# Norm statistics of a two-block fp32 kernel: squares summed in four column groups instead of by full-width products or by VectorE adds

## The reference

```python
def layer_norm(x, g, b):
    xf = x.astype(jnp.float32)
    mu = jnp.mean(xf, axis=-1, keepdims=True)
    var = jnp.mean(jnp.square(xf - mu), axis=-1, keepdims=True)
    y = (xf - mu) * lax.rsqrt(var + LN_EPS)
    return (y * g.astype(jnp.float32) + b.astype(jnp.float32)).astype(x.dtype)
...
        x = layer_norm(ALPHA * x + 0.5 * swiglu(x, ffn1_w1[i], ffn1_w3[i], ffn1_w2[i]), ln1_g[i], ln1_b[i])
        proj = x @ w_in[i]
...
        x = layer_norm(ALPHA * x + merged @ w_out[i], ln2_g[i], ln2_b[i])
        x = layer_norm(ALPHA * x + 0.5 * swiglu(x, ffn2_w1[i], ffn2_w3[i], ffn2_w2[i]), ln3_g[i], ln3_b[i])
        ple = jax.nn.sigmoid(x @ ple_w_gate[i]) * (p[i] @ ple_w_proj[i])
        x = layer_norm(ALPHA * x + ple, ln4_g[i], ln4_b[i])
...
        h = rms_norm_2(x, norm_g[l]) * (1.0 + scale) + shift
```

## Time and profile before

| | us |
|---|---|
| median of 3 runs | 3131.28 (3130.58 to 3132.92) |
| profiled execution, its time | 3131.53 |
| profiled execution, its span | 3129.7 |
| mean granted clock of PE, share of full | 0.998 |
| busy: PE, DVE, ACT | 3082.8, 2368.0, 1222.6 |

### The profile page before, as it was taken

One profiled execution on the slowest core, in us unless ns is written; L12 is line 12 of the kernel. 1 busy time (PEld: TensorE's weight loads), 2 busy tenths in 40 slices (PEclk: granted clock), 3 DMA queues, 4 the chain that ended last, 5 costly groups with the idle time before them and its releaser, 6 DMA issues.

```text
span 3129.7 us, 37552 instructions
## 1 busy us (share of the span) xinstructions
PE 3082.8 (98%) x14712; PEld 2490.4 (80%) x14712; DVE 2368.0 (76%) x4017; ACT 1222.6 (39%) x1884; POOL 56.2 (2%) x49
## 2 busy tenths in 40 slices
PE   8999999999999999999999999999999999999998
PEld 6887888877988887777878888888777788788887
DVE  6777767778869678888598776767797789789736
ACT  4233323335342455554243233222366534534414
POOL 0000000000000001130000000000000000000000
PEclk9999999999999999999999999999999999999999
DMA  3222212223343351012212111111211221122242
GB/s 131 74 73 75 81 61 68 68 68 109 119 101 135 115 197 56 8 48 114 95 54 68 41 54 61 48 54 48 68 54 63 104 77 64 48 70 101 81 168 74
DMA packets 89247, 250.13 MB, mean 80 GB/s; under 512 B 8560, under 2 KB 24816, under 8 KB 87536
## 3 DMA queue, kind: packets, MB, share of 16 engines
q1 hardware_dynamic: 89072, 247.73, 23.5%
HBM read 203.65 MB, written 44.04 MB: 79 GB/s over the span
## 4 chain that ended last, share of the span: by engine, by line
PE 90%; DVE 7%; ACT 2%; issue 1%; DMA 0%; DVEq 0%; SPq 0%; ACTq 0%
PE PS L577 88%; PE PS L582 2%; DVE WS L2228 1%; DVE X L2236 1%; DVE XS L2236 1%; DVE HELD L2290 1%; DVE X L2228 1%; ACT XS L1345 0%; DVE COLB L3038 0%; DVE XSf L2228 0%; ACT XSf L1345 0%; DVE TMP L2228 0%; DMA RAW<-in_W 0%; DVE TMP L2232 0%; ACT WS L1345 0%
## 5 line engine op out<-in xcount | busy, mean ns | idle before, releaser
L577 PE MATMUL PS<-XS,WS 128*128 128x512 f32 (+1 forms) x6480 | 1513.8, 391 | 20.4 <-DVE XS L2228 9.5
L577 PEld LDWEIGHTS PS<-XS,WS 128*128 128x128 f32 x6480 | 1208.9, 188 | 297.8 <-issue 27.1
L577 PE MATMUL PS<-HS,WS 128*128 128x512 f32 x2208 | 511.0, 390 | 3.1 <-DVE TMP L2228 2.7
L577 PEld LDWEIGHTS PS<-HS,WS 128*128 128x128 f32 x2208 | 414.1, 188 | 93.1 <-DVE TMP L2228 3.5
L2228 DVE TENSOR_TENSOR WS<-RAW,WS 128x512 fp32r<-128x512 f32 (+1 forms) x398 | 346.9, 880 | 173.8 <-ACT WS L1345 173.2
L1345 ACT ACTIVATE WS<-RAW 128x512 fp32r<-128x512 f32 (+1 forms) x398 | 307.6, 779 | 398.7 <-PE PS L577 344.0
L2228 DVE TENSOR_TENSOR X<-PS,X 128x512 f32<-128x512 f32 x272 | 184.2, 688 | 101.8 <-PE PS L577 101.7
L2228 DVE TENSOR_TENSOR TMP<-TMP,PS 128x512 f32<-128x512 f32 x304 | 203.6, 682 | 61.5 <-PE PS L577 58.7
L577 PE MATMUL PS<-T,WS 128*128 128x512 f32 x960 | 230.6, 389 | 0.0
L577 PEld LDWEIGHTS PS<-T,WS 128*128 128x128 f32 x960 | 180.2, 188 | 37.4
L1345 ACT ACTIVATE TMP<-PS 128x512 f32<-128x512 f32 x144 | 85.0, 596 | 291.0 <-PE PS L577 274.4
(11 more groups left out here) (338 smaller groups left out, 3580.6 us busy)
## 6 DMA issues: line engine op xcount, KB each, us to landing
RAW<-in_W SPq DMA_DIRECT2D x263, 512.0 KB, 3.3
RAWX<-in_W SPq DMA_DIRECT2D x30, 512.0 KB, 3.3
DC<-TMP SPq DMA_DIRECT2D x32, 256.0 KB, 2.1
X<-in_xT SPq DMA_DIRECT2D x8, 512.0 KB, 8.9
DX<-X SPq DMA_DIRECT2D x2, 2048.0 KB, 8.4
DCZ<-CA SPq DMA_DIRECT2D x8, 512.0 KB, 4.1
DGA<-TMP SPq DMA_DIRECT2D x16, 256.0 KB, 2.3
DGB<-TMP SPq DMA_DIRECT2D x16, 256.0 KB, 3.1
```

What stands on the lines that cost most here:

```text
L577: done = d.matmul(out, l, r, start=first, stop=last)
```

## The change

All ten half-norms now sum their squares in the same way, with no adds on DVE. For each k-tile, four products (`quarter_sums`) each take a quarter of the tokens (128 columns) with 32 columns of `ones` and write rows 32g to 32g+31 and columns 0 to 127 of the bank. After eight k-tiles, row group g holds the sums of quarter g. The root and the reciprocal (`rstd_rows`) then work on 128 columns instead of 512, in a TMP tile. Four further f32 products (`spread`) bring them back: column 32g of the identity, repeated 128 times, picks the row of quarter g and writes it to all rows, columns 128g on, of the same bank. DVE's scalings read that bank instead of HELD or HX, so the bank is free only at the last scaling (y7). The steps of `side` are one more, so the hooks are moved, and HX is gone.

```diff
-SUMMED = ("ln1", 1), ("ln2", 0), ("ln2", 1), ("ln3", 1), ("ln4", 0)
...
     SQ = [at(f"SQ{k}", 154 + 4 * k, [128, 512], F32) for k in range(8)]
     GW = at("GW", 188.0625, [128, 3, 128], F32)
-    HX = at("HX", 184, [128, 2, 512], F32)
...
             for k in range(8):
-                if within and k == 4:
+                if within and k in within:
                     hook()
...
+        def quarter_sums(out, src, first, last):
+
+            return mms([(out[32 * g:32 * g + 32, 0:128], ones[:, 0:32], src[:, 128 * g:128 * g + 128], first, last)
+                        for g in range(4)])
+
+        def spread(name, h):
+
+            r = tmp("rs", name, h)
+            e.wait_ge(ve("rs", name, h), dma("const")("cols"))
+            mms([(var_bank(name, h)[:, 128 * g:128 * g + 128], ident[:, 32 * g:32 * g + 1].to_broadcast([128, 128]), r[:, 0:128], True, True)
+                 for g in range(4)]).then_inc(*mm.inc("rb", name, h))
+
         def norm(name, h):
             mean, var = (name, "mean", h), (name, "var", h)
...
-            banks.take(var, (ac, "rs", name, h))
-            yield
-            if (name, h) in SUMMED:
-                yield
-                e.wait_ge(ve(name, "sqs", 7, h), *banks.free(var))
-                mms([(bank(*var), ones[:], squares(name, 0, h), True, True)]).then_inc(*mm.inc(name, "var", 7, h))
-            else:
-                e.wait_ge(*banks.free(var))
-                for k in range(8):
-                    if k == 4:
-                        yield
-                    e.wait_ge(ac(name, "sq", k, h))
-                    mms([(bank(*var), ones[:], squares(name, k, h), k == 0, k == 7)]).then_inc(*mm.inc(name, "var", k, h))
-            yield
-            yield
+            banks.take(var, (ve, name, last_scaled(name), 7, h))
+            yield
+            e.wait_ge(*banks.free(var))
+            for k in range(8):
+                if k == 4:
+                    yield
+                e.wait_ge(ac(name, "sq", k, h))
+                quarter_sums(bank(*var), squares(name, k, h), k == 0, k == 7).then_inc(*mm.inc(name, "var", k, h))
+            yield
+            spread(name, h)
             yield
...
-                product8(us[m], h, use, "ln3", beside=True, within=n in (1, 2, 3, 8, 9, 10, 12) or None)
+                product8(us[m], h, use, "ln3", beside=True,
+                         within={1: (4,), 2: (4,), 3: (4, 7), 8: (4,), 9: (4,), 10: (4, 7), 12: (4, 7)}.get(n))
...
-                        if k == 4 and h == 0 and i < 2:
+                        if k == 4 and h == 0 and i in (0, 1, 2, 4):
                             next(steps)
...
-            tmps.take(use, (ve, *(end or use)))
+            tmps.take(use, (mm, "rb", name, h) if width == 128 else (ve, *(end or use)))
...
-            root(name, h, 1024, LN_EPS, mm(name, "var", 7, h))
+            root(name, h, 1024, LN_EPS, mm(name, "var", 7, h), width=128)
...
+        def rstd_rows(name, h):
+
+            r = tmp("rs", name, h)[:, 0:128]
+            e.wait_ge(ac("rs", name, h))
+            d.reciprocal(r, r).then_inc(*ve.inc("rs", name, h))
+
...
-            if (name, h) in SUMMED:
-                total = squares(name, 0, h)
-                for k in range(1, 8):
-                    e.wait_ge(ac(name, "sq", 0, h), ac(name, "sq", k, h), *([ve(name, "sqs", k - 1, h)] if k > 1 else ()))
-                    tt(total, total, squares(name, k, h), ALU.add).then_inc(*ve.inc(name, "sqs", k, h))
-            yield
-            e.wait_ge(ve(name, "c", 7, h))
-            rstd(name, h, s)
+            yield
+            rstd_rows(name, h)
             yield
...
-                e.wait_ge(ve("rs", name, h), ac(name, "sq", 7, h))
-                scaled = stt(x, x, col(name + "_g", k), s, ALU.mult, ALU.mult)
+                e.wait_ge(mm("rb", name, h), ac(name, "sq", 7, h), ve(name, "c", 7, h))
+                scaled = stt(x, x, col(name + "_g", k), var_bank(name, h), ALU.mult, ALU.mult)
```

More of the change, by code:

```diff
@@ L481, in var_bank, with last_scaled @@
         return bank(name, "var", h) if name in LNS else bank("sq", name, h)
+    def last_scaled(name):
+        return "y0" if name == "ln4" else "y"
     def out_part(p):
@@ L643, in merge_norm @@
             yield
-            banks.take(var, (ac, "rs", "ln2", h))
-            e.wait_ge(ve("ln2", "sqs", 7, h), *banks.free(var))
-            mms([(bank(*var), ones[:], squares("ln2", 0, h), True, True)]).then_inc(*mm.inc("ln2", "var", 7, h))
+            banks.take(var, (ve, "ln2", "y", 7, h))
+            e.wait_ge(*banks.free(var))
+            for k in range(8):
+                e.wait_ge(ac("ln2", "sq", k, h))
+                quarter_sums(bank(*var), squares("ln2", k, h), k == 0, k == 7).then_inc(*mm.inc("ln2", "var", k, h))
+            yield
+            spread("ln2", h)
             yield
@@ L680, in up @@
                         banks.take(use3, (ve, name, "mul", fi, h))
-                        product8(us[fi][0], h, use1, tag, within=h == 0)
+                        product8(us[fi][0], h, use1, tag, within=None if h else (4, 7) if fi else (4,))
                         product8(us[fi][1], h, use3, tag, within=None if h == 0 else False)
@@ L777, in latents @@
                 for k in range(8):
-                    if k == 4 and n in (1, 2, 3):
+                    if k == 4 and n in (1, 2, 3) or k == 7 and n == 3:
                         hook()
@@ L1104, in out_product @@
                 banks.take(use, (ve, *use))
-                product8(u, h, use, "mh", pair=mh_pair, beside=h == 1, within=m in (3, 6) and h == 1 or None)
+                product8(u, h, use, "mh", pair=mh_pair, beside=h == 1, within={3: (4,), 6: (4, 7)}.get(m) if h else None)
             us = [w.take() for _ in range(8)]
@@ L1119, in norm_h @@
             steps = norm("ln4", h)
-            for _ in range(3):
+            for _ in range(4):
                 next(steps)
                 yield
-            square_sum("h", h, 8, lambda k: SQ[k][:])
+            use = ("sq", "h", h)
+            banks.take(use, (ve, "hy", 7, h))
+            e.wait_ge(*banks.free(use))
+            for k in range(8):
+                e.wait_ge(ac("sq", "h", h, k))
+                quarter_sums(bank(*use), SQ[k], k == 0, k == 7).then_inc(*mm.inc("sq", "h", h, k))
+            yield
+            spread("h", h)
             yield
@@ L1966, in embed @@
             biased(0)
-            root("h", 0, 1024, RMS_EPS, mm("sq", "h", 0, 7))
+            root("h", 0, 1024, RMS_EPS, mm("sq", "h", 0, 7), width=128)
             gate(12)
@@ L2064, in mixer @@
                     biased(1)
-                    root("h", 1, 1024, RMS_EPS, mm("sq", "h", 1, 7))
+                    root("h", 1, 1024, RMS_EPS, mm("sq", "h", 1, 7), width=128)
                     for k in range(8):
@@ L3149, in part @@
                     ALU.add, ALU.subtract).then_inc(*ve.inc("xs", "h", k, h))
-            rstd("h", h, HX[:, h, :])
+            rstd_rows("h", h)
             for k in range(8):
-                e.wait_ge(ve("gc", 1), ve("rs", "h", h), ac("ln4", "y", k, h), *tmps.free(("hp", h, k)))
-                stt(tmp("hp", h, k), X[:, k, half(h)], GC[:, 0, k:k + 1], HX[:, h, :], ALU.mult, ALU.mult).then_inc(
+                e.wait_ge(ve("gc", 1), mm("rb", "h", h), ac("ln4", "y", k, h), *tmps.free(("hp", h, k)))
+                stt(tmp("hp", h, k), X[:, k, half(h)], GC[:, 0, k:k + 1], var_bank("h", h), ALU.mult, ALU.mult).then_inc(
                     *ve.inc("hy", k, h))
```

## The result

The kernel after takes 3144.84 us (median of 5 runs, 3144.33 to 3145.67) against 3131.7 us of the kernel before in the same session (5 runs). The ratio is 1.0042, with a 95% interval of 1.0027 to 1.0056: slower by 13.1 us. Its profiled execution took 3144.84 us (span 3142.9), so it stands for the median, and its span is 13.2 us over that of before.

A forecast was written before the change was run, and what follows sets the result against it. TensorE (PE), busy 98% of the span, was taken to bound the kernel. Terms 0 + 0.7 + 2.5 + 0.2 - 0.1 + 15.6 + 2.5 - 8.0 = +13.4 us on 3131.53 gave about 3145 us, range 3136 to 3158.

The forecast's parts named there:

- places 1: ln1 half 0, first ffn: last down group stands 4.9 us for y7, waits that go offset it; sum 0.
- place 5: ln3 half 0, second ffn: first gate product waits for y7, but waits for XS parts go; -0.1 us.
- place 6: ln3 half 1, gate stage: 11.5 us stop at n = 5 for y7, plus 2.7 for the clock; +15.6 us in all.
- place 7: ln4 and h half 0: dearer ln4 sums, cheaper h sums, PE standing about 3.1 us at the spread; +2.5 us.
- variant (E): Rival: the clock also falls at ln1 half 0 and ln3 half 0, +2.5 to +5 us; inside the main case's 0.62.
- place 2: ln1 half 1, latents: +2.9 us of PE work minus four waits of 2.6 in all, perhaps a spread wait; +0.7 us.
- Quarter sums and spread: Unit costs on PE: 1.4 us for 4 k-tiles, 2.4 for 8 in a row, 1.03 for a spread.
- place 3: ln2 half 0, merge: sums and spread dearer for PE, no wait before to give back; +2.5 us.
- places 2 and 4: 4 is ln2 half 1: +2.5 us minus about 2.3 of waits, +0.2; place 2 was +0.7.
- Place 8: ln4 and h half 1, last norm: shorter reciprocals and sums on the chain over DVE; -8.0 us.
- Rival (C): Quarter sums: only two column groups at once, +1.4 us at some six places, +8, 3153 us; chance 0.13.
- Rival (B): Quarter sums: column groups run one after another, each sum 4.3 us more, +35, 3180 us; chance 0.05.

The follow-up runs named there:

- skip5: Kernel after with one bank of the ring left out ahead of the gate product of n = 5: 3130.11 us, ratio to before 0.9996.
- warm: Kernel after with 48 useless products right ahead of the 11.1 us stop at n = 5: 3142.66 us, ratio to before 1.0034.
- recip3: Kernel before with the change at ln4 and h half 1 alone, their 128-column reciprocals made three times in a row: 3125.28 us, ratio to before 0.9979.
- gouter: Kernel after with quarter products of ln1, ln3 and ln4 issued one column group after the other: 3162.1 us (a single run).
- h0_late3: Kernel after, banks left out at n = 0 and n = 5, spread of h half 0 moved 18 products later: 3123.94 us, ratio to before 0.9975.
- last_only: Kernel before with the change made for ln4 half 1 and h half 1 alone: 3122.81 us, ratio to before 0.9972.
- skip3: Kernel after with banks left out at n = 0 and n = 5 (the one meant at ln1 was not): 3129.27 us, ratio to before 0.9992.

## Why the prediction was right, and where its steps were off

The time was 3144.84 where 3145 was said, and the sign and the chain were right, but that it came within 0.2 us is luck: the slow clock was 5.5 us more than its term, place by place the other terms were too dear by some 4 us, and 1.7 us came from stretches that the change doesn't touch.

**The wait for the bank (places 1, 5, 6).** Right. The stops at places 1 and 6 were predicted at 4.9 and 11.5 us and were 4.65 and 11.14; the one at place 5, for which no length was given, was 2.14, and the 1.99 us for the spread there were not in the prediction at all. Without the slow clock the two cost nothing, as its -0.1 has it. skip5 shows that place 6 is the bank. The working of y7 there, held by a weight part that waits for PE, holds too: in after VectorE stands 5.00 us idle between the reciprocal and this weight part, which ACT delivers late, having itself waited 4.89 us for PE:

```profile
2301.49 0.95 DVE L2316 RECIPROCAL TMP<-TMP 128x128 f32<-128x128 f32 x1 [1.65 <-ACT TMP L1365]
2307.44 1.23 DVE L2248 TENSOR_TENSOR WS<-RAW,WS 128x1024 fp32r<-128x1024 f32 x1 [5.00 <-ACT WS L1365]
2308.58 1.40 DVE L2256 SCALAR_TENSOR_TENSOR X<-X,COL,PS 128x512 f32<-128x512 f32 x2
...
2323.39 0.74 DVE L2256 SCALAR_TENSOR_TENSOR X<-X,COL,PS 128x512 f32<-128x512 f32 x1
```

**The clock (places 1, 5, 7).** This is the term that was too small. I counted it once, 2.7 us at place 6; it was 2.3 there (warm shows it apart), but also 2.5, 1.7 and 1.7 us behind the stops of 4.65, 2.14 and 3.81 us: 8.2 in all. I had the case for places 1 and 5 as variant (E) and left place 7 out. I also didn't see that the trace of before has such a piece itself, at 752 us in place 2.

**Quarter sums and spread.** Too dear. What a block costs has to be counted as the 6.9 us of the full sum were, with the tenths that its neighbours lose to it: from one block's start to the next with 12 products between them it is 3.95 us (2423.41 to 2427.36), so 1.23 us a block, of which 1.01 is its own. Eight k-tiles cost 1.88 and the same 0.22, so 2.1, and a spread 0.9. My sum for four groups at once gave 1.25 and 2.1, and the rows bear it out: 32 more instructions cost 0.87 us (1.01 to 1.88), so 0.027 each, a quarter of 0.104, and 0.36 is left for both switches where I had 0.4. The step that failed is the one behind it, where I took 1.4 and 2.4 to be nearer to the rate of two groups; the spread was 0.13 too dear too. That is 0.4 us at place 3, and as much or more at 2, 4 and 8. Rival (C), two groups at a time, is excluded by the 1.01 us.

**The waits that were to go (place 2).** Of four waits, 2.6 us in all, I expected none. In after three are left, 1.06, 0.39 and 0.39 us, for parts of XS. That place 2 came out at 0.2 us all the same, against a kernel before with full clock there, is, as far as the rows can be added up, owed to the cheaper sums and to the tenths that each stop costs beside its idle time, which I had left out (recip3).

**Rival (B) and the overlap rule.** The Trainium skill, "TensorE: Matmul & The Clock Gate", Part 3 (What overlaps and what doesn't), has weight loads overlap running products only where the row group differs. The 1.01 us a block, with one row group throughout, disagrees with a serial reading of it, and the measurement decides. gouter lies nearer to the rule, with 0.074 us an instruction where neighbours share the column group as well. The same part has 2.38x for three column tiles. Here a full sum of 6.9 us became 2.1, 3.3x for four. By tile that is 0.82 beside 0.79, so the trace agrees, with 128 moved columns where the page's row has 512.

**Place 7.** The stop ahead of the spread was 3.81 us where I said 3.1: since the sums and the earlier spread were cheaper than I had them, PE came to it sooner, while ACT's root (at 2387.78) stood behind the eight biased rows and a table load. Moving the spread behind 18 more products gave back what the place had cost: 63.12 us from mean to mean in h0_late3, 63.09 in before.

**VectorE's work.** It fell by 45 us where I said some 60: by the records 35 adds of 0.69 us and ten reciprocals 2.4 us shorter are 48. Outside the last norm it shows only in the waits that went at places 2 and 4.

**Place 8.** -8.8 where I said -8.0, alone -8.9 in last_only. The chain from the mean to y(h) became 29.3 us (2446.23 - 2416.97), where I had 30.05; the terms given for that number, taken whole, make about 27, and how much of the sums lies on the chain was left to judgement. PE's own work had the larger say: in after it waits only 0.36 us at the first part of XS.

**A stretch that nothing touches** gave 1.5 us between 763 and 1550. Two stops that both kernels have (1.94 us at 1095 in after, 1.33 us at 1450 in before) were each followed by a lower clock in one trace and not in the other, so they cancel. What is left is a wait at 1132, put down to instruction issue, which was 0.92 us instead of 2.33. It is no part of the change: in the other traces the wait there is between 0.55 and 2.4 us, with the same code around it.

## What to carry to other kernels

A PSUM bank that is read at the end of a chain instead of at its start comes free later, and the ring may come round before that: before moving an operand into PSUM, count the takes up to the next owner of that bank, and price the stop with the slow products behind it. One bank left out of the turn can be worth more than the whole change, but it moves all later owners, so the phase has to be restored where it doesn't hurt. And a change made at ten alike places should be judged at each: here one place earned nearly 9 us, one lost 14.5.

## What the runs showed of the hardware

- **The clock behind short stops varies between executions.** Stops of 2.0 to 2.1 us were followed by products at 1.2 GHz in some executions (after at 2272.86, skip3 at 2259.90: 1.7 us lost) and at 2.4 GHz in others (skip5, both stops; gouter at 2281.99, behind 2.56 us). A stop of 2.0 us at 67 to 68 us, ahead of anything that the kernels differ in, stands in all thirteen traces, and in six of them the granted clock behind it was 0.50. The stops of 3.81, 4.65 and 11.14 us in after were followed by the lower clock, at 1.7 to 2.5 us each. What decides it for the short ones stays open.
- **Filling a stop with work that nobody needs can pay**: 48 products in the stop of 11.1 us made the kernel 2.2 us faster. No shorter stop was filled.
- **Four column groups in turn** cost 0.027 us an instruction of 128 columns, a quarter of a full-width one (0.104), with 0.36 us for both switches; in a row of one group 0.074.
- **A stop costs more than its idle time**: 2.35 us in recip3 for two stops of 1.8 us together, at full clock.
